# First two layers: the attention's output product over all heads at once, after the last head

## The reference

```python
mod = silu_c @ ada_w[i] + ada_b[i]                # six modulation vectors of a layer
h = rms_norm(x, norm_mix_g[i]) * (1.0 + sc1) + sh1
# layer 0, differential attention:
a = p[:, 0] - lam_full * p[:, 1]                  # two softmax maps of a head
o = einsum('bhqk,bkhe->bqhe', a, v)
o = rms_norm(o, subln_g) * (1.0 - lambda_init)    # layer 0 alone: a norm per head
y = o.reshape(B, S, D) @ w_o                      # W_o, 1024 x 1024
# layer 1, chunked attention: the same without the norm
x = x + g1 * y
h = rms_norm(x, norm_ffn_g[i]) * (1.0 + sc2) + sh2
x = x + g2 * grouped_moe(h, ...)
```

## Time and profile before

| what | value |
|---|---|
| median of 3 runs | 1739.26 us |
| profiled execution, its time | 1736.32 us |
| profiled execution, span from first to last instruction | 1734.5 us |
| PE busy | 1617.4 us, 93% of the span |
| DVE busy | 473.0 us, 27% |
| ACT busy | 368.1 us, 21% |
| mean rate over the span, from HBM | 308 GB/s |

### The profile page before, as it was taken

The page is one execution under the profiler, slowest core; times in us unless marked ns, Lnnn a source line. Parts: engine busy times, 40 slices in busy tenths (PEclk is TensorE's granted clock), DMA queues, the critical chain, the costliest instruction groups (busy, mean ns, idle before and its releaser), DMA issues.

```text
span 1734.5 us, 20614 instructions
## 1 busy us (share of the span) xinstructions
PE 1617.4 (93%) x8418; PEld 901.9 (52%) x8418; DVE 473.0 (27%) x1118; ACT 368.1 (21%) x770; POOL 34.0 (2%) x44
## 2 busy tenths in 40 slices
PE   5999879999989988999998996897799999999998
PEld 3664654444465647444444782345644444444444
DVE  2044331212123234312122123463311212121212
ACT  2142221111122234211112311442211111111111
POOL 0000000000000000000000001040000000000000
PEclk9999989999999998999999996897799999999999
DMA  9996649999999567699998100004269999999995
GB/s 320 386 386 246 245 166 427 428 429 428 414 335 331 194 243 321 281 427 428 428 429 329 49 1 0 1 1 194 97 286 425 429 429 429 429 429 428 428 427 238
DMA packets 94672, 535.17 MB, mean 309 GB/s; under 512 B 7935, under 2 KB 11737, under 8 KB 69922
## 3 DMA queue, kind: packets, MB, share of 16 engines
q1 hardware_dynamic: 94258, 534.41, 75.8%
q10 hardware_dynamic: 368, 0.12, 0.0%
HBM read 533.44 MB, written 1.06 MB: 308 GB/s over the span
## 4 chain that ended last, share of the span: by engine, by line
PE 85%; DMA 5%; DVE 4%; SPq 2%; ACT 2%; issue 1%; DVEq 0%; POOL 0%; ACTq 0%
PE pair L901 24%; PE bank L890 7%; PE pair L908 6%; PE bank L630 6%; PE bank L908 6%; DMA ring<-in_w_dram 4%; PE bank L637 3%; PE bank L591 3%; PE bank L951 3%; PE pair L951 3%; PE bank L724 2%; SPq L403 1%; DMA ring<-in_a_w_qkv_dram 1%; PE bank L1047 1%; PE pair L1112 1%
## 5 line engine op out<-in xcount | busy, mean ns | idle before, releaser
L901 PE MATMUL pair<-ring,arena 128*64 128x512 f32 x2048 | 447.3, 594 | 3.5 <-DVE arena L1837 2.9
L901 PEld LDWEIGHTS pair<-ring,arena 128*64 128x64 f32 x2048 | 144.7, 137 | 288.1 <-issue 288.1
L890 PE MATMUL bank<-arena 128*128 128x128 f32 x1120 | 139.5, 279 | 9.4 <-DVE arena L1825 9.4
L1850 DVE TENSOR_TENSOR arena<-sq,pair 128x512 f32<-128x512 f32 x32 | 34.0, 1061 | 408.2 <-PE pair L901 408.2
L890 PEld LDWEIGHTS bank<-arena 128*128 128x128 f32 x1120 | 133.6, 196 | 9.9 <-issue 9.9
L630 PE MATMUL bank<-hh,ring 128*128 128x256 f32 x512 | 120.6, 394 | 6.9 <-ACT hh L1206 3.5
L908 PE MATMUL pair<-ring,arena 128*64 128x512 f32 x512 | 116.9, 598 | 0.0
L908 PE MATMUL bank<-ring,arena 128*64 128x512 f32 x512 | 115.3, 592 | 0.0
L630 PEld LDWEIGHTS bank<-hh,ring 128*128 128x128 f32 x512 | 99.4, 197 | 28.0 <-issue 11.6
L1376 ACT ACTIVATE sq<-pair 128x512 f32<-128x512 f32 x32 | 19.1, 597 | 370.3 <-PE pair L901 370.3
L1858 DVE COPY arena<-bank 128x512 f32<-128x512 f32 x32 | 22.1, 692 | 202.7 <-PE bank L908 202.7
(11 more groups left out here) (375 smaller groups left out, 1623.3 us busy)
## 6 DMA issues: line engine op xcount, KB each, us to landing
ring<-in_w_dram SPq DMA_DIRECT2D x96, 2048.0 KB, 15.6
ring<-in_moe_w_gate_dram SPq DMA_DIRECT2D x32, 2048.0 KB, 11.6
ring<-in_moe_w_up_dram SPq DMA_DIRECT2D x32, 2048.0 KB, 15.9
ring<-in_moe_w_down_dram SPq DMA_DIRECT2D x32, 2048.0 KB, 13.9
ring<-in_ada_w_dram SPq DMA_DIRECT2D x24, 2048.0 KB, 17.4
ring<-in_w_mod_dram SPq DMA_DIRECT2D x12, 2048.0 KB, 12.2
ring<-in_a_w_qkv_dram SPq DMA_DIRECT2D x6, 2048.0 KB, 19.2
ring<-in_b_w_qkv_dram SPq DMA_DIRECT2D x6, 2048.0 KB, 11.7
```

Source lines behind the costliest of these rows:

```text
L890: last = mm(b[part][:, cols(k % 4)], h_tok[:, t, cols(k)], pick[:, t, :], start=(t == 0), stop=(t == TT - 1))
L901: last = mm(b[2 + m][half(a), :], x_sel[:, k, half(a)], R8[moe_slot(l, a, m)][:, k, :], start=(k == 0), stop=(k == KT - 1))
L1850: tt(hid.rearrange("p (f q) -> p q f", f=FT), by_row(gate_act), by_row(b[3]), ALU.mult).then_inc(M["hid_ready"], 1)
```

## The change

In layers 0 and 1 the pieces `out_first` and `half_out` go. W_o becomes one product over all eight blocks after the last head, by the function that layer 2 uses, through the banks 0 to 3. Both chunks of W_o go to the end of the layer's list, behind all eight of `B`. On PE `transposes(4)` now stands ahead of `scores(6)`, `values(h)` each moves ahead of the next transposes, and `mods_turn` goes ahead of `values(7)`. On ACT `mods_copy` goes ahead of `head_out(7)`, and on DVE `mods_add` goes ahead of `out_scale(1)`.

```diff
-            add_mods(B[0], B[1], B[2], B[3])
-            add_out(l, 0, 16 * l + 8)
-            add_mods(B[4], B[5], B[6], B[7])
-            add_out(l, 1, 16 * l + 16)
+            add_mods(*B)
+            add_out(l, 0, 8 * l + 8)
+            add_out(l, 1, 8 * l + 8)
 ...
                 scores(5)
                 mods(B[3])
-                out_first(0)
+                transposes(4)
                 scores(6)
-                transposes(4)
                 mods(B[4])
-                out_first(1)
+                values(4)
+                transposes(5)
                 scores(7)
-                transposes(5)
-                values(4)
                 mods(B[5])
-                out_first(2)
+                values(5)
                 transposes(6)
-                values(5)
                 mods(B[6])
-                out_first(3)
+                values(6)
                 transposes(7)
-                values(6)
                 mods(B[7])
-                out_first(4)
+                mods_turn(2 * l + 2)
                 values(7)
-                out_first(5)
                 if l == 0:
                     out_sums(1)
-                out_first(6)
-                out_first(7)
-                mods_turn(2 * l + 2)
-                if l == 0:
                     out_spread(1)
-                for c in range(KT):
-                    out_second(c)
-                square_sum(KT - 2)
-                square_sum(KT - 1)
-
-            def project_out(src):
-                ws_ = [R4[slot_of_chunk(out_at[2][n])] for n in range(2)]
+                    pe.wait_ge(norm_ready, 24)
+                pe.wait_ge(o_ready, heads + 8)
+                pe.wait_ge(s_added, heads + 8)
+                project_out(l, oT)
+
+            def project_out(l, src):
+                ws_ = [R4[slot_of_chunk(out_at[l][n])] for n in range(2)]
                 for n in range(2):
-                    chunk_in(out_at[2][n])
+                    chunk_in(out_at[l][n])
                 for c in range(KT):
                     if c >= 4:
-                        pe.wait_ge(x_attn, 16 + c - 3)
+                        pe.wait_ge(x_attn, 8 * l + c - 3)
                     for k in range(KT):
                         last = mm(b[c % 4][:, 0:S], ws_[k // 4][:, k % 4, cols(c)], src[:, k, :],
                                   start=(k == 0), stop=(k == KT - 1))
 ...
# ScalarE
                 head_out(6)
+                mods_copy(2 * l + 2)
                 head_out(7)
                 if l == 0:
                     out_root(1)
-                mods_copy(2 * l + 2)
 ...
# VectorE: half_out(0) to half_out(7) go
                 weights(7)
+                mods_add(2 * l + 2)
                 if l == 0:
                     out_scale(1)
-                mods_add(2 * l + 2)
-                if l == 0:
                     out_normed(1)
-                for c in range(KT):
-                    ...
+                add_out(l)
```

More of the change, by code:

```diff
@@ L253, in program @@
         turn_ps, probT_ready, pv_ps, o_ready = (sem(n) for n in ("turn_ps", "probT_ready", "pv_ps", "o_ready"))
-        out_proj, x_half, x_attn = sem("out_proj"), sem("x_half"), sem("x_attn")
+        out_proj, x_attn = sem("out_proj"), sem("x_attn")
         logits_ps, h_turned, h_tok_ready = sem("logits_ps"), sem("h_turned"), sem("h_tok_ready")
@@ L338, in program @@
             chunks.append((columns(QKV[2], n), in_proj, done))
-        add_out(2, 0, 32 + 8)
-        add_out(2, 1, 32 + 8)
+        add_out(2, 0, 24)
+        add_out(2, 1, 24)
         moe_at.append(len(chunks))
@@ L710, in values @@
                     last.then_inc(pv_ps, 1)
-                def out_first(c):
-                    if c == 0:
-                        pe.wait_ge(o_ready, heads + 4)
-                        if l == 0:
[L716 to L729, removed]
-                        if l == 0:
[L731 to L744, removed]
                 for i in range(4):
@@ L1179, in _ @@
             hybrid()
-            project_out(ymix)
+            project_out(2, ymix)
             route(2)
@@ L1663, in weights @@
                     last.then_inc(prob_ready, 1)
[L1665 to L1668, removed]
                 head_scale(8)
@@ L1692, in attention_layer @@
                 maxima(5)
-                half_out(0)
                 weights(4)
                 maxima(6)
-                half_out(1)
                 weights(5)
                 maxima(7)
-                half_out(2)
                 weights(6)
-                half_out(3)
                 weights(7)
-                half_out(4)
-                half_out(5)
+                mods_add(2 * l + 2)
                 if l == 0:
                     out_scale(1)
-                half_out(6)
-                half_out(7)
-                mods_add(2 * l + 2)
-                if l == 0:
                     out_normed(1)
-                for c in range(KT):
[L1713 to L1716, removed]
+                add_out(l)
             def add_out(l):
                 for c in range(KT):
-                    dve.wait_ge(out_proj, 16 * l + c + 1)
+                    dve.wait_ge(out_proj, 8 * l + c + 1)
                     stt(xT[:, c, :], b[c % 4][:, 0:S], mod[:, l, G1 + c:G1 + c + 1], xT[:, c, :],
```

## The result

The changed kernel takes 1746.74 us (median of six runs, 1745.48 to 1751.16) against 1739.15 us (six runs, 1736.14 to 1740.77): 7.6 us more, ratio 1.0049, 95% interval 1.0035 to 1.0063. By the interval that is 6.1 to 11.0 us. The forecast was 1743.7 (+4.4), rival A 1747.3 (+8.0). The profiled execution has a span of 1744.5 us, 10.0 more than the one of before. That is more than 7.6 because the profiled execution of before was a quick one: 1736.32 us, 2.8 under the median of the six, while that of the changed kernel lies 0.5 under its own.

A forecast was written before the change was run, and what follows sets the result against it. PE was taken to bound the kernel, with a loop over DVE nearly as long. Layer 0 +1.55, layer 1 +0.65 and the clock +2.2 sum to +4.4 us on 1739.26, giving 1743.7 us; range 1738 to 1749.

The forecast's parts named there:

- rival A: Ahead of W_o in both layers: the clock falls and comes back late, +8.0 us, 1747.3 us; chance 0.26.
- PE's work does not change, 13.8 us leave the heads: Both layers: same matmuls, but 32 of them at 0.431 us, 13.8 us, move from among the heads to behind them.
- Heads of layer 0, 5.40 us a head: Layer 0, after B[3]: the loop over DVE takes 5.40 us a head against PE's own 3.99, idling PE 1.4.
- The norm's chain, 7.6 us, W_o 29.66 us behind the start of B[3]: Layer 0, behind values(7): the norm loses its cover, W_o starts at 191.98, layer 0 costs +1.55 us.
- ACT's table load, 1.28 us: Layer 0's norm: the load takes 1.28 us without a drain, against the skill page's about 2.66 us.
- Layer 1, W_o held by the last chunk until 25.34 us behind B[3]: Layer 1: W_o waits for its second chunk, landing at 641.0, and starts at 641.1; costs +0.65 us.
- The clock, one fall in layer 0 for 2.2 us, likeliest none in layer 1: Ahead of W_o: one fall in layer 0, bounds 0 to 2.9 us, taken as 2.2; likeliest no fall in layer 1.
- Other edits at nothing: half_out's removal counted in the loop, banks nothing, later expert tiles hidden behind router and gate product; range 0 to +0.5 us.
- Rival B: Both layers: no fall of the clock at all, +2.2 us, 1741.5 us; chance 0.18.
- Rival C: Among the heads: the loop over DVE is no limit, PE runs 3.99 us a head; -2.0 us, 1737.3 us; chance 0.05.
- rival D: Layer 1's last chunk lands in time and no clock falls: sum -0.05 us, 1739.2 us; chance 0.09.

The follow-up runs named there:

- e1: Changed kernel plus matmuls nobody reads in PE's idle ahead of W_o, nine in layer 0 and six in layer 1: 1738.22 us, ratio 1.0007 to the kernel before.
- e8: The changed kernel run once more, unedited: 1744.01 us, ratio 1.0035 to the kernel before.
- e10: Changed kernel plus six matmuls nobody reads behind values(7) in layer 1 alone: 1741.62 us, ratio 1.0024 to the kernel before.
- e5: Changed kernel with PE's wait for W_o's second chunk moved to its first use, the fifth matmul: 1740.84 us, ratio 1.0017 to the kernel before.
- e3: The change in layer 1 alone, layer 0 with the code of before: 1741.44 us, ratio 1.0018 to the kernel before.
- e9: Changed kernel plus nine matmuls nobody reads around out_spread(1) in layer 0 alone: 1742.97 us, ratio 1.0029 to the kernel before.
- e6: Kernel before with half_out placed behind the weights on DVE among heads 4 to 7: 1722.35 us, ratio 0.9908 to the kernel before.
- e2: The change in layer 0 alone, layer 1 with the code of before: 1741.15 us, ratio 1.0049 to the kernel before.

## Why the prediction was right or wrong

The direction came as forecast, the size did not. The time lies just above the forecast's own 1741 to 1746.5 us and at rival A, and the outcome that I held likeliest, no more than 0.3% of change (0.58), is not what came: slower by more had 0.37. The step that failed is the clock in layer 1.

- *PE's work does not change, 13.8 us leave the heads:* right. Same count, and at full clock (e1) the product with its sums takes 31.0 us, 72 x 0.431. The 64 records of the earlier trace rows are two for each matmul, not a load and a matmul as I read them; that they are 32 matmuls stays.
- *Heads of layer 0, 5.40 us a head:* right. In e8, where the clock stayed up among them, transposes(4), (5) and (6) stand at 166.02, 171.31 and 176.60, 5.29 apart. PE idles 2.0, 1.2 and 1.2 us ahead of them:

```profile
166.02 0.55 PE L693 MATMUL pair<-cst,arena 128*128 128x128 f32 x3 [2.03 <-DVE arena L1618]
...
171.31 0.55 PE L693 MATMUL pair<-cst,arena 128*128 128x128 f32 x3 [1.18 <-DVE arena L1618]
...
176.60 0.55 PE L693 MATMUL pair<-cst,arena 128*128 128x128 f32 x3 [1.18 <-DVE arena L1618]
```

  In layer 1 of the changed kernel they are 5.10 apart (forecast 5.20).
- *The norm's chain, 7.6 us, W_o 29.66 us behind the start of B[3]:* 30.1 in the profile, 29.5 in e8 (162.06 to 191.54). The heads ended 0.2 to 0.4 us earlier than forecast (values(7) start 21.9 and 21.6 us behind B[3], not 22.03), although the clock fell among them in the profile, which I had not counted and which cost 0.3. The chain behind them was longer, 8.3 us in the profile and 7.9 in e8: the clock falls inside it already, and the four spreads take 1.24 and 0.88 us, where at full clock they take 0.71 (e10, whose chain is 7.7).
- *ACT's table load, 1.28 us:* right; in the changed kernel it starts at 185.43 and the root at 186.72, 1.29 behind it. The Trainium skill's 2.66 us (page "ScalarE: Activation LUTs", section "What ACT_TABLE_LOAD costs") would, as an estimate, have put the root at 188.1; the measurement decides.
- *Layer 1, W_o held by the last chunk until 25.34 us behind B[3]:* right to 0.1 us (25.27), and e5 shows the cause.
- *The clock, one fall in layer 0 for 2.2 us, likeliest none in layer 1:* this step failed, in its second half. The fall came in layer 1 too, in all four profiles with the wait for the transfer unfilled (the changed kernel, e3, e8, e9), and cost 2.4 to 2.6 us; the one in layer 0 cost 3.0 (2.3 in e8). I had held against it that values(7), a full product, lies in the stretch; it did not help. That is rival A, mechanism and place, at 1747.3 us. The sum was made for the profiled execution, and there +10.0 us stand against +4.4. Of the 5.6 missing, 2.4 are the fall that I left out in layer 1, 0.8 the size of the one in layer 0, 0.4 W_o's later start there, 1.5 the router and first gather behind layer 0, where I had nothing, and 0.5 what is left. Most of that 1.5 is clock as well: the router's small products (L830 to L833, from 242.95) start 0.43 to 0.45 us apart, where those of before (from 237.91) start 0.22 to 0.24 apart. Neither the forecast nor rival A names this place. By the medians only 3.0 us are missing, because the profiled execution of before, from which all rows come, was 2.8 us quicker than the usual one. That this offsets part of the error, and that 1747.3 comes so near 1746.74, is luck.
- *Other edits at nothing:* nothing in the traces speaks against it; the down tiles were not waited for.
- *Rival B's argument,* that idle pieces of 1.4 to 2.2 us leave the clock up: true of the profile that I had, not of every execution. In e3 the same code loses the clock there.
- *Rival C* falls with the spacing of 5.29; *rival D* with the wait on the transfer.
- What I did not draw from the earlier trace rows, though it stood there: the 1.37 to 2.2 us of idle a head did not belong to the early product but to the order of two instructions on DVE. The change moved the product away and got 11.8 (layer 0) and 13.2 us (layer 1) of the 13.8 back; the order alone takes 16 us off the kernel (e6).

## What to carry to other kernels

Where an engine idles because its producer does something else first, swap the two in the producer's list before moving the work: the early half product was good cover, held back by one addition. Work that is moved behind the last dependency takes its cover along; ask what lies beside each remaining step, and price the clock of TensorE for every stretch in which it would do little. Filling such a stretch with real matmuls that are ready (half of the sum, in free banks) beats leaving it idle, and so did matmuls whose result nobody reads.

## What the runs showed of the hardware

- TensorE's clock fell to 1.2 GHz behind 2.0 us of idle (changed kernel, 166 us) and 2.2 us (e3, 182 us), and in other executions of the same code it did not (e8, where the windows from 164 to 170 us show 1.00). The same idle is free in one execution and costs in the next. In e5 it was down from 645.0 to 648 us, some 0.4 us into W_o, behind idle pieces of only 0.7 and 0.5 us with the turn's small products and values(7) between them.
- A fall in front of W_o cost 1.4 to 3.0 us of its 31.0 us, in layer 0 (3.0 in the changed kernel, 2.8 in e5, 2.6 in e10, 2.3 in e8, 1.4 in e2) as in layer 1 (2.6 in e8 and e9, 2.5 in e3, 2.4 in the changed kernel, 1.7 in e5). It came in every profile in which that stretch was left unfilled: in layer 0 some 7 us from the end of values(7), with small sums and spreads in it, in layer 1 some 5 us from the end of B[7], with values(7) in it (3 us in e5).
- A fall may cost nearly nothing: the one at 167 us halved the pace of the product for B[4] (3.51 us for 1.85) but moved the next transposes by 0.3 us, since in e8, without the fall, PE idled 1.18 us ahead of them.
